# Layer one's mixing by two and three tiles, its merge, output, second norm and queries in three groups

## What is computed

```python
def layer(x, c, ...):
    sh1, sc1, g1, sh2, sc2, g2 = split(silu(c) @ w_mod + b_mod, 6)
    h = rmsnorm(x, ln1_w) * (1 + sc1) + sh1
    x = x + g1 * token_mixer(h, ...)
    h = rmsnorm(x, ln2_w) * (1 + sc2) + sh2
    return x + g2 * peer(h, wq, k1, k2, u, v)

def token_mixer(h, ...):
    z, xbc, dt, lx, ly, g_ssd, g_lru = split(h @ w_in)
    y_ssd = rmsnorm(ssd_scan(silu(conv(xbc)), dt, ...) * silu(z))     # scan over tokens
    y_lru = rglru(conv(lx)) * gelu(ly)                                # scan over tokens
    merged = sigmoid(g_ssd) * (y_ssd @ w_br_ssd) + sigmoid(g_lru) * (y_lru @ w_br_lru)
    return merged @ w_out

def peer(h, ...):          # 8 heads, top 16 of 128 keys twice, top 16 of the 256 sums
    act = gelu(h . u[e]) * g        # 128 experts of 16384 for each token
    return sum(act * v[e])
```

## Time and profile before

| | us |
|---|---|
| median of three runs | 4469.14 |
| lowest and highest | 4463.95, 4475.38 |
| the profiled execution, its own time | 4474.27 |
| its span | 4472.5 |

### The profile page before, as it was taken

How to read it: one execution, slowest core, us unless ns; L and a number is a source line. 1 busy time by engine, 2 the same in 40 slices (tenths; PEclk the granted TensorE clock), 3 DMA queues, 4 the chain that set the end, 5 groups by cost and what they waited for, 6 DMA issues and landing times.

```text
span 4472.5 us, 62170 instructions
## 1 busy us (share of the span) xinstructions
PE 3195.3 (71%) x22770; PEld 1896.7 (42%) x22770; DVE 2828.3 (63%) x6601; ACT 1497.2 (33%) x4707; POOL 1455.9 (33%) x1298
## 2 busy tenths in 40 slices
PE   7899956888997644498988758879987444444443
PEld 4456844565554322254566535555544221111111
DVE  2422177875457977776754697875459885585554
ACT  2215114436223222444632325364232222232222
POOL 0000013322443344344433333323432444444342
PEclk9999977899998755599999878889998655555555
DMA  8343459999999999999999999989999899999997
GB/s 322 138 156 124 130 223 360 352 362 357 401 418 372 364 388 419 404 373 402 416 418 417 416 386 368 380 336 403 416 407 355 350 421 419 421 419 420 421 421 331
DMA packets 285244, 1610.96 MB, mean 360 GB/s; under 512 B 61786, under 2 KB 66704, under 8 KB 117900
## 3 DMA queue, kind: packets, MB, share of 16 engines
q0 software_dynamic: 184320, 1342.26, 73.5%
q1 hardware_dynamic: 80656, 256.81, 15.4%
q10 hardware_dynamic: 19964, 7.91, 0.6%
HBM read 1597.63 MB, written 7.91 MB: 359 GB/s over the span
## 4 chain that ended last, share of the span: by engine, by line
DMA 25%; PE 24%; DVE 20%; ACT 7%; issue 4%; POOL 2%; ACTq 0%; DVEq 0%; POOLq 0%; SPq 0%
DMA ring<-in_peer_uv,units 24%; PE psum L672 16%; DVE ring L1968 8%; PE psum L1067 5%; POOL ring L659 2%; DVE both L1830 1%; ACT diag L1438 1%; PE psum L1089 1%; DVE best L1836 1%; DVE best L1829 1%; DVE places L1829 1%; DVE best L1833 1%; DVE places L1836 1%; ACT L1320 1%; DVE best L1826 1%
## 5 line engine op out<-in xcount | busy, mean ns | idle before, releaser
L659 POOL DMA_INDIRECT ring<-in_peer_uv,units x1280 | 1452.7, 1135 | 2980.5 <-PE psum L1067 2135.7
L1968 DVE SCALAR_TENSOR_TENSOR ring<-ring,hrow 128x1024 f32<-128x1024 f32 x1280 | 1538.9, 1223 | 869.6 <-DMA ring<-in_peer_uv,units 811.7
L1067 PE MATMUL psum<-ring,diag 128*32 128x256 f32 x10240 | 922.5, 493 | 1021.2 <-ACT diag L1438 1020.9
L672 PE MATMUL psum<-hT,wslot 128*128 128x384 f32 (+1 forms) x4224 | 1249.6, 452 | 10.7 <-ACT hT L1153 3.1
L672 PEld LDWEIGHTS psum<-hT,wslot 128*128 128x128 f32 x4224 | 820.3, 198 | 418.5 <-issue 88.6
L1067 PEld LDWEIGHTS psum<-ring,diag 128*32 128x32 f32 x10240 | 327.5, 131 | 1547.3 <-ACT diag L1438 1207.7
L1428 ACT ACTIVATE gel<-hid 128x2 f32<-128x2 f32 x640 | 129.2, 202 | 1768.1 <-DVE ring L1968 1753.2
L672 PE MATMUL psum<-region,wslot 128*128 128x256 f32 (+1 forms) x1536 | 442.4, 442 | 4.7 <-ACT region L1326 3.6
L672 PEld LDWEIGHTS psum<-region,wslot 128*128 128x128 f32 x1536 | 290.7, 193 | 140.6 <-issue 26.0
L1438 ACT ACTIVATE diag<-pick,wgt 128x32 f32<-128x32 f32 x1280 | 331.7, 306 | 0.0
L1432 ACT ACTIVATE wgt<-gel,units 128x1 f32<-128x1 f32 x1280 | 307.3, 287 | 20.9
(11 more groups left out here) (247 smaller groups left out, 2815.8 us busy)
## 6 DMA issues: line engine op xcount, KB each, us to landing
wslot<-in_w_tiles SPq DMA_DIRECT2D x360, 512.0 KB, 7.6
ring<-in_w_modt SPq DMA_DIRECT2D x24, 2048.0 KB, 9.1
ring<-in_peer_uv,units POOLq DMA_INDIRECT x1280, 14.1
wslot<-in_w_gate SPq DMA_DIRECT2D x32, 128.0 KB
region<-in_states_t SPq DMA_DIRECT2D x16, 256.0 KB, 10.9
region<-in_states_n SPq DMA_DIRECT2D x16, 256.0 KB, 11.3
out_new_ssd_sample<-region ACTq DMA_DIRECT2D x16, 256.0 KB, 17.5
xT<-in_x_t SPq DMA_DIRECT2D x1, 2560.0 KB, 9.4
```

The source lines that it names most:

```text
L659: pool.indirect_dma_start(ring[:, n, :], None, table, bass.IndirectOffsetOnAxis(ap=units[:, s % 2, block, 0, quad:quad + 1].bitcast(U32), ...
L672: last = pe.matmul(out, wslot[:, n % SLOTS, k * P:(k + 1) * P], src(k), start=k == 0, stop=k == KT - 1)
L1067: last = pe.matmul(psum[c * BLOCK:(c + 1) * BLOCK, block % 2, block // 2 * 256:(block // 2 + 1) * 256], diag[:, n, :], ring[:, n, D + c * ...
L1968: dve.scalar_tensor_tensor(out=ring[:, n, 0:D], in0=ring[:, n, 0:D], scalar=1.0, in1=hrow[:, e % 2, :], op0=ALU.mult, op1=ALU.mult, accum_ ...
```

## The change

Layer 0 is cut in another way; layer 1 keeps its tiles. Regions are now five, described by tables: which tiles a region mixes, merges and queries, and any of the first two may be absent.

```diff
-FIRST, COUNT = (0, 3), (3, 2)
-T0 = (0, 3 * P)
-NG = (3 * P, 2 * P)
-PN = (3 * P, P)
-REGIONS = 2 * DEPTH
-CUT = (2, 2)
...
+LAYER = (0, 0, 0, 1, 1)
+MIX = ((0, 2), (2, 3), None, (0, 3), (3, 2))
+MERGE = ((0, 2), (2, 1), (3, 2), (0, 2), (2, 3))
+ASK = ((0, 2), (2, 1), (3, 2), (0, 2), (2, 3))
+REGIONS = len(LAYER)
...
-EARLY = 2
+EARLY = OPENS[1]
...
-    window(first[-2:] + pairs_of(2)[:12], steps_of(1)[half[1]:], 0, 12)
-    window(pairs_of(2)[12:50], [], 0, 1)
-    window(pairs_of(2)[50:], [(EARLY, i - BASE[EARLY]["X"]) for i in range(BASE[EARLY]["X"])], 1, 13)
-    window(pairs_of(3, 4)[:124], steps_of(2)[:half[2]], 9, 124)
-    window(pairs_of(3, 4)[124:] + pairs_of(5)[:12], steps_of(2)[half[2]:], 0, 14)
...
+    window(first[-2:] + pairs_of(2)[:10], steps_of(1)[half[1]:], 0, 11)
+    window(pairs_of(2)[10:], steps_of(2)[:half[2]], 0, 46)
+    window(pairs_of(3)[:9], steps_of(2)[half[2]:] + [(EARLY, i - BASE[EARLY]["X"]) for i in range(BASE[EARLY]["X"])], 0, 9)
+    window(pairs_of(3, 4)[9:124], steps_of(3)[:half[3]], 0, 115)
+    window(pairs_of(3, 4)[124:] + pairs_of(5)[:12], steps_of(3)[half[3]:], 0, 14)
...
 def choice_at(t):
-    return PAIRS * (t - 1) + {1: 30, 3: 14, 4: -20, 6: 30, 8: 16, 9: 16}.get(t, 8)
+    return PAIRS * (t - 1) + {1: 30, 4: 14, 6: 30, 8: 16, 9: 16}[t]
 def passes(s):
-    return 2 if s in TILE0 else 1
+    return 2 if s in (0, 2, 3, 5, 7) else 1
```

More of the change, by code:

```diff
@@ L121, in share @@
     name = max((BASE[r][name], name) for name in SHARE if BASE[r][name] <= i)[1]
-    tiles = out_count(r) if i >= BASE[r]["M"] else COUNT[r % 2]
-    return SHARE[name] * (0.75 if tiles == 2 and name not in ("S", "N1", "N2") else 1)
+    tiles = ASK[r][1] if i >= BASE[r]["Q"] else out_count(r) if i >= BASE[r]["M"] else COUNT[r]
+    return SHARE[name] * ({1: 0.5, 2: 0.75, 3: 1}[tiles] if name not in ("S", "N1", "N2") else 1)
 TAKE_OUT, TURN_OUT, ADD = (2, 3), (3, 5), (4, 6)
@@ L201, in weight_positions @@
     for r in range(REGIONS):
-        for name, count in (("X", 10), ("Z", 8), ("LX", 8), ("LRU", 16), ("M", 32), ("OUT", 8), ("Q", 16)):
+        for groups, name, count in ((MIX, "X", 10), (MIX, "Z", 8), (MIX, "LX", 8), (MIX, "LRU", 16), (MERGE, "M", 32), (MERGE, "OUT", 8), (ASK, "Q", 16)):
             pos[r, name] = n
-            n += count
+            n += count if groups[r] else 0
+    pos["all"] = n
     return pos
 POS = weight_positions()
-LOADS = 98
 def loads_in(r, i):
@@ L235, in same_group @@
 def same_group(s):
-    return s % NT not in (CUT[s // NT] - 1, NT - 1)
+    return s + 1 < TILES_E and s + 1 not in TILE0
 def within(s):
@@ L291, in chosen @@
 def chosen(r):
-    return PH * sum(out_count(u) for u in range(r))
+    return PH * sum(ASK[u][1] for u in range(r))
 def build(nc, a):
@@ L471, in __init__ @@
                 self.mixed, self.m1 = room(S_AT, KT, N), room(S_AT + KT * ROW, N)
-                self.qT = room(S_AT, 2, 2, N)
-                if self.sample:
+                if self.tails:
                     self.tail_rows = room(S_AT + 3456, 5, 512)
-        G = (Mixing(0), Mixing(1))
-        O = [Output(r) for r in range(REGIONS)]
+        class Asking:
+            def __init__(self, r):
+                first, self.nt = ASK[r]
+                self.N, self.t0, self.sample = self.nt * P, first * P, first + self.nt == NT
+                self.qT = room(S_AT, 2, 2, self.N)
+        G = [Mixing(r) if MIX[r] else None for r in range(REGIONS)]
+        O = [Output(r) if MERGE[r] else None for r in range(REGIONS)]
+        K = [Asking(r) for r in range(REGIONS)]
         def of_norm(n):
-            return O[n // 2] if n % 2 else G[n // 2 % 2]
+            return O[n // 2] if n % 2 else G[n // 2]
         cin = room(0, KT, 9)
@@ L545, in weights @@
                     for r in range(REGIONS):
-                        l, g = divmod(r, 2)
-                        if g == 0:
+                        l, closes = LAYER[r], r in CLOSES
+                        if r in OPENS:
                             small_ones(l)
[L549 to L552, removed]
-                                    mod_chunk(c)
-                            if r == 0 and 4 <= j < 8:
-                                mod_chunk(4 + j)
@@ L556, in weights @@
[L556 to L580, removed]
+                        if MIX[r]:
+                            for j in range(10):
+                                yield load(tile(l, TX + j))
+                                if r == 0 and j == 3:
+                                    for c in range(4, 8):
+                                        mod_chunk(c)
+                                if r == 0 and 4 <= j < 8:
+                                    mod_chunk(4 + j)
+                            if r == 0:
+                                for c in range(12, 16):
+                                    mod_chunk(c)
+                            for j in range(8):
+                                if closes and j == 4:
+                                    states(l, range(13))
+                                yield load(tile(l, TZ + j))
+                                if r == 0 and j >= 4:
+                                    mod_chunk(12 + j)
+                            for j in range(8):
+                                yield load(tile(l, TLX + j))
+                                if r == 0 and j < 4:
+                                    mod_chunk(20 + j)
+                                if closes and j < 3:
+                                    states(l, (13 + j,))
+                            for j in range(8):
+                                yield load(tile(l, TLY + j))
+                                yield load(a["w_gate"].rearrange("l k p c -> p (l k) c")[:, l * KT + j, :], 2 * P)
@@ L581, in weights @@
+                        if MERGE[r]:
+                            for j in range(8):
+                                for first in (TGS, TBS, TGL, TBL):
+                                    yield load(tile(l, first + j))
+                            if r in OPENS:
+                                keys(l)
+                            for j in range(8):
+                                yield load(tile(l, TOUT + j))
                         for j in range(16):
@@ L597, in _ @@
                 for e, steps in PLAN:
-                    while n < min(taken + SLOTS, REGIONS * LOADS):
+                    while n < min(taken + SLOTS, POS["all"]):
                         next(ahead)
```

385 lines of the change are left out of this document (220 added, 165 removed).

## The result

The change is slower: 4537.4 us (median, 4536.0 to 4538.9) against 4472.3 of the kernel before beside it, a ratio of 1.014 (95% interval 1.0124 to 1.0155). The prediction had 4476 and a range to 4520. (The "layer one" of the title is the first layer, the text's layer 0.) The profiled execution has a span of 4536.1 us, 63.6 more than the one before.

A forecast was written before the change was run, and what follows sets the result against it. TensorE was taken to bound the kernel before the first pair, the 16 DMA engines after it. Terms -77 - 41 + 86 + 8 + 28 + 3 = +7 gave a median of 4476 us, own range 4456 to 4483, 8-in-10 range 4424 to 4520.

The forecast's parts named there:

- step 6: Tile 3 split into two passes, four more turned rows and copies per tile: +3 us (0 to 8).
- The head: Region 0, before the first expert pairs, mixes two tiles, not three: -77 us (ends -70 and -88).
- Pairs 16 to 138: Layer 0's next mixing (460 us), merge and output (202), queries (145): sum 807, -41 us (ends -75 and 0).
- the bytes: Transfer time summed: 5.0 us per pair, 1.25 per weight load, plus gate loads and states; 289 in layer 0's mixing.
- Pairs 138 to 198: Tile 2's pairs, no longer bare, beside merge, output and queries of tiles 3 and 4: +86 us (+68 to +98).
- The early norm: Layer 1's early norm, 12 steps sharing nine pairs with eight query steps: +8 us (0 to +20).
- Tile 4's choice: Choice of experts moved to pairs 206 to 234, beside layer 1's x and SSD: +28 us (0 to +44).
- the DVE decides: Slower rival: serial DVE work beside mixing stalls gathers; +67 us, 4536, half of it 4506; chance 0.24.
- The DVE has room: Faster rival: tile 4's choice and early norm cost nothing, mixing at 1.05; -59 us, 4410, half 4440; chance 0.33.
- Costlier loads: Slower rival: each of tile 2's 56 added loads costs 1.46 us, not 1.25; +12 us, 4488; chance 0.07.

## Why the prediction was wrong, step by step

The forecast was +7 us of span, and 63.6 came. The largest single error is step 6: of the 57 us in its two stretches the moved choice explains 31 and the forecast had 3 more, so 23 are missing, and without them the span would have been some 4513, inside the range. The rest is spread over steps 2 to 5, with 8 us given back by the head and by what lies behind pair 256.

1. *The head*: -77 forecast, -79.8 measured. Right, with its parts: TensorE was the bound and the loads did not take it back.

2. *Pairs 16 to 138*: -41 against -25.5. Merge and output 202 against 200.1; mixing 460 against 473.1; queries 145 against 154.9. The border of this stretch had been read 6 us early (1564.7; the first dot of pair 138 is at 1570.5), which hid part of the miss. The DVE's work was summed right: 351 us forecast for mixing, 350.8 measured, at a busy share of 74%. But the reading of mixing's excess lacked a part. I gave the 56 us over the bytes to the DVE, the states and the choice; tile 0 is a two-pass tile, and setting its halves apart gave back 17 us in one execution of the kernel before and 7 in another. The layer 1 stretch that I compared with lies beside tile 3, in one pass, a difference that I didn't see. What the remaining excess is made of no run shows.

3. *Pairs 138 to 198*: +86 against +104.5, of which 6 are that border. Merge and output were right, 215 against 217.8, with some luck: the sum of bytes was taken as the only bound, and PE's work was a second one, 15 us below it. The queries were mis-sized, 173 against 183. They were sized from a stretch of 30 pairs in which they spread evenly; here 14 of their 22 steps stand in 14 pairs and eight bare pairs follow. But spreading them brought nothing, thin loads brought nothing, setting the halves apart brought 2 us and halving the matmuls 6. Why the queries cost 10 us more than sized stays open.

4. *The early norm*: +8 against +12.9. The prediction spreads its steps over nine pairs; the plan puts all twelve in pairs 199 and 200. Packed alone, four to a pair, they cost 6 in place; the rest is not isolated.

5. *Tile 4's choice*: +28 forecast, +30.7 alone. Right, and by the mechanism named: 42 us of DVE work that was free beside bare pairs costs 31 us beside mixing. By the prediction's own border the stretch took 216 us in that run with the DVE 84% busy, where it had 209 at 87%.

6. *Tile 3's two passes*: "+3 (0 to 8)" is the step that failed, and its upper end with it. Alone they cost 37 us (15.5 and 21.2 in two stretches); with the moved choice both cost 57 in those stretches, less than their sum of 67. The prediction priced the added instructions, four turned rows and copies, and put the wait that each carries at nothing. That wait, PE's second half behind ACT's copy of the first, was 27 of the 37 us, and the added work some 8 to 10. Two-pass tiles do run as fast as others beside bare pairs (tile 2's take 5.0 us a pair, those of tile 8, in one pass, 5.05), but tile 3 is beside mixing, where the slack is gone. A row of the page before the change showed the wait, 123.0 us of PE idle ahead of line 1089, and the prediction passes over it.

The rival *the DVE decides* was right about the sign and about step 5's mechanism, though it priced the choice at 44 us and mixing at 492, against 31 and 473. It had nothing on the passes; its price, +67, is close to the result by chance. *The DVE has room* fell with the cost of the choice. *Costlier loads* fell too: thinning the 56 loads gave back 15 us in merge and output and none in the queries.

## What to carry to other kernels

When a change moves work beside other work, price the waits of every instruction added as well as its busy time, and ask for each stage that looked cheap what gave it the slack. Two stretches that are compared should be alike in everything that the plan decides for them: here one had one pass and the other two. Where two engines hand halves of a job back and forth through one buffer in a fixed order, leave slots between the hand-overs. Here the second half had followed the first by one pair; four pairs between them were worth 0.65% before the change and 1.4% after it, in one line.

## What was not expected of the hardware

Nothing in the units themselves. Between pairs 94 and 106 after the change, a 128-column projection takes PE 1.95 to 2.05 us where the granted clock is 1.00 and 3.78 us where it is 0.50, as the prediction had taken from its rows, and the one-tile merge ran at 418 GB/s. What surprised was how near the bounds lie: beside tile 2's experts bytes alone give 210 us by the sum, PE is busy 197, and taking away 21 MB of the stretch's loads gained 15 us, half of PE's matmuls another 30.
